# Router products from chunks of x2 inside the branch stage, with the root and the offset applied afterwards

## The reference, cut to what matters

```
x  = x + g1 * (merged @ w_out)                       # x2, 320 x 1024
h2 = rms_norm(x, norm2_w) * (1 + sc2) + sh2          # sc2, sh2 per sequence
logits = h2 @ w_router + b_router                    # 320 x 32
top_val, top_idx = top_k(logits, 4)
top_w = softmax(top_val)
y  = sum over the 4 experts of top_w * expert(h2)    # clamped SwiGLU, 32 experts
x  = x + g2 * y ; then a final RMSNorm
```

## Time and profile before

| | |
|---|---|
| median of 3 runs | 1829.15 us (1824.63 to 1832.14) |
| the profiled execution's own time | 1827.68 us |
| its span | 1825.7 us |
| PE busy | 1624.7 us (89%) |
| DVE busy | 766.2 us (42%) |
| ACT busy | 410.9 us (23%) |
| POOL busy | 126.7 us (7%) |

### The profile page before, as it was taken

One profiled execution on the slowest core, in us unless ns is written; L12 is line 12 of the kernel. 1 busy time (PEld: TensorE's weight loads), 2 busy tenths in 40 slices (PEclk: granted clock), 3 DMA queues, 4 the chain that ended last, 5 costly groups with the idle time before them and its releaser, 6 DMA issues. The chain is left out here.

```text
span 1825.7 us, 24039 instructions
## 1 busy us (share of the span) xinstructions
PE 1624.7 (89%) x8449; PEld 872.7 (48%) x8450; DVE 766.2 (42%) x1531; ACT 410.9 (23%) x792; POOL 126.7 (7%) x208
## 2 busy tenths in 40 slices
PE   6997898899978999878998988999989999899995
PEld 3775584686855676564333333333323333333332
DVE  2355332344152001284446265364462653644626
ACT  3234112111001200123223133132231331312313
POOL 0211120211210420010000000000000000000000
PEclk9899998999589999978999999999999999999997
DMA  9362208113018533305989999999999999999991
GB/s 314 143 221 74 74 1 314 55 47 104 0 46 243 193 131 146 138 1 238 424 356 425 426 416 425 412 425 425 415 425 417 414 424 393 425 426 409 426 401 43
DMA packets 115088, 494.61 MB, mean 271 GB/s; under 512 B 9947, under 2 KB 27548, under 8 KB 65831
## 3 DMA queue, kind: packets, MB, share of 16 engines
q1 hardware_dynamic: 113050, 491.21, 67.4%
q10 hardware_dynamic: 1984, 2.64, 0.5%
HBM read 487.39 MB, written 6.43 MB: 270 GB/s over the span
## 5 line engine op out<-in xcount | busy, mean ns | idle before, releaser
L761 PE MATMUL ps_mix<-hT,ring 128*128 128x320 f32 x896 | 263.7, 452 | 19.4 <-DVE ring L1234 9.7
L761 PEld LDWEIGHTS ps_mix<-hT,ring 128*128 128x128 f32 x896 | 175.7, 199 | 99.1 <-issue 16.4
L1905 PE MATMUL ps_moe<-ring,hT_moe 128*64 128x512 f32 x672 | 157.2, 627 | 2.6 <-ACT hT_moe L1848 2.6
L1905 PE MATMUL ps_moe<-ext,xg 128*64 128x512 f32 x672 | 147.0, 594 | 0.4 <-issue 0.2
L1905 PE MATMUL ps_moe<-ring,xg 128*64 128x512 f32 x672 | 147.1, 594 | 0.0
L2091 DVE TENSOR_SCALAR hid<-ps_moe 128x256 f32<-128x256 f32 (+1 forms) x96 | 48.8, 509 | 154.4 <-ACT hid L1840 111.5
L2077 DVE TENSOR_SCALAR gate<-ps_moe 128x1024 f32<-128x1024 f32 x32 | 39.2, 1225 | 148.5 <-ACT hid L1835 99.9
L1905 PEld LDWEIGHTS ps_moe<-ring,hT_moe 128*64 128x64 f32 x672 | 54.4, 145 | 98.3 <-issue 97.9
L2063 DVE TENSOR_TENSOR work<-work,ps_moe 128x640 f32<-128x640 f32 x128 | 99.4, 818 | 1.4 <-PE ps_moe L1921 0.3
L1905 PEld LDWEIGHTS ps_moe<-ext,xg 128*64 128x64 f32 x672 | 48.3, 137 | 94.2 <-issue 91.9
L1905 PEld LDWEIGHTS ps_moe<-ring,xg 128*64 128x64 f32 x672 | 47.1, 137 | 91.0 <-issue 91.0
(11 more groups left out here) (409 smaller groups left out, 2225.0 us busy)
## 6 DMA issues: line engine op xcount, KB each, us to landing
ext<-in_w_gate SPq DMA_DIRECT2D x128, 1024.0 KB, 15.6
ring<-in_w_up SPq DMA_DIRECT2D x128, 1024.0 KB, 15.9
ring<-in_w_down SPq DMA_DIRECT2D x128, 1024.0 KB, 12.2
ring<-in_w_in SPq DMA_DIRECT2D x18, 2048.0 KB, 8.3
ring<-in_w_ada SPq DMA_DIRECT2D x12, 2048.0 KB, 10.9
ext<-in_state_gdn_rec SPq DMA_DIRECT2D x8, 512.0 KB, 7.3
out_rec_sample<-ext SPq DMA_DIRECT2D x8, 512.0 KB, 6.1
ring<-in_w_branch_b SPq DMA_DIRECT2D x2, 2048.0 KB, 10.3
```

Of the source, the lines that this page charges most:

```text
L761: last = nc.tensor.matmul(out, ring[:, place(i), k, P * j:P * j + P], rhs[:, k, :], start=k == 0, stop=k == NC - 1)
L1905: ends = [nc.tensor.matmul(ps[MID * a:MID * a + MID, bank + blk, :], lhs(blk, c), w[:, k, HALF * a:HALF * a + HALF], start=c == 0 and not ...
```

## The change

PE no longer multiplies h2T with the router's matrix. In the branch stage DVE makes, for each chunk, x2 times its weights w (`hx`, kept in the place of `gb`), and PE multiplies these chunks with `wr` on the four strips: four products after unit 4 of `wo`, four after the last unit and ahead of the last square. After the reciprocal DVE multiplies the result by `rstd` into the first chunk of `yacc` (which is `lrow` now; the copy by ACT is gone). In the routing stage PE forms sh2 @ w_router for the nine sequences (`shw`), and adds it to the tokens with `seqT`, a 0/1 matrix of sequence by token that POOL makes first. The prompt's offset of h2 is added by ACT instead of DVE. POOL clears `yacc` in the routing stage, after the logits.

```diff
 # branches
+        def logits(c0):
+            pe.wait_ge(hx_s, c0 + NSTRIP + HX0)
+            for q in range(NSTRIP):
+                last = nc.tensor.matmul(ps[STRIP * q:STRIP * q + STRIP, 6, 0:T], wr[:, c0 + q, :], hx[:, c0 + q, :],
+                                        start=c0 == 0, stop=c0 > 0)
+            last.then_inc(lg_t, 1)
...
             if kind == "wo" and c >= 1:
                 add_square(c - 1)
+            if (kind, c) == ("wo", NSTRIP):
+                pe.wait_ge(ld, 32)
+                logits(0)
+        logits(NSTRIP)
         add_square(NC - 1)
...
+                if c == 0:
+                    link(nc.vector.tensor_scalar(gw2[:], SC2, 1.0, None, ALU.add))
+                    nc.vector.tensor_tensor(gw2[:], gw2[:], n2w.unsqueeze(2).to_broadcast([P, NC, NSEQ]), ALU.mult).then_inc(gw_s, 1)
...
+                dve.wait_ge(dve_s, taken(n)[1])
+                nc.vector.tensor_scalar(hx[:, c, 0:SEQ], x2T[:, c, 0:SEQ], gw2[:, c, 0:1], None, ALU.mult)
+                nc.vector.tensor_tensor(seq_view(hx[:, c, SEQ:T]), seq_view(x2T[:, c, SEQ:T]),
+                                        gw2[:, c, 1:NSEQ].unsqueeze(2).to_broadcast([P, NS, ST]), ALU.mult).then_inc(hx_s, 1)
...
         nc.vector.reciprocal(rstd[:], rstd[:]).then_inc(rs_s, 1)
+        dve.wait_ge(rs_s, 2)
+        dve.wait_ge(lg_t, 2)
+        nc.vector.tensor_tensor(yacc[:, 0, :], ps[:, 6, 0:T], rstd[:], ALU.mult)
 # experts, POOL
+                nc.gpsimd.memset(seqT, 1.0).then_inc(seq_s, 1)
...
+                nc.gpsimd.affine_select(out=seqT[:, 0:SEQ], in_=seqT[:, 0:SEQ], compare_op=ALU.is_equal, fill=0.0,
...
+                pool.wait_ge(lg_t, 3)
+                nc.gpsimd.memset(yacc[:], 0.0)
 # experts, ACT
-                nc.scalar.activation(lrow[:], ps[:, 6, 0:T], ACT.Copy).then_inc(lrow_s, 1)
+                for c in range(NC):
+                    act.wait_ge(hm_s, 9 * 16 + c + 1)
+                    nc.scalar.activation(h2T[:, c, 0:SEQ], h2T[:, c, 0:SEQ], ACT.Identity, bias=SH2[:, c, 0:1]).then_inc(h_s, 1)
 # experts, PE
+                for c in range(NC):
+                    last = nc.tensor.matmul(ps[0:NSEQ, 0, 0:E], SH2[:, c, :], wr[:, c, :], start=c == 0, stop=c == NC - 1)
+                last.then_inc(shw_t, 1)
...
+                    nc.tensor.matmul(o, lrow[:, t0:t0 + n], expert_row[:], start=True, stop=False)
+                    last = nc.tensor.matmul(o, seqT[:, t0:t0 + n], shw, start=False, stop=True)
...
+                        if tau == 0:
+                            pe.wait_ge(h_s, k + 1)
 # experts, DVE
+                dve.wait_ge(shw_t, 1 + SHW0)
+                nc.vector.tensor_copy(shw, ps[0:NSEQ, 0, 0:E]).then_inc(shw_s, 1)
...
-                        nc.vector.tensor_scalar(h2T[:, c - 1, 0:SEQ], h2T[:, c - 1, 0:SEQ], SH2[:, c - 1, 0:1], None,
-                                                ALU.add).then_inc(h_s, 1)
```

More of the change, by code:

```diff
@@ L1239, in branches @@
 def branches(nc, t, st, sb, sem, ring, ident, ones, gnw, short, adaT, hT, oT, zT, tails, x2T, xrow, order, norm, load_slot,
-             wait_slot, load_piece, yacc, brow, rstd, wr, br):
+             wait_slot, load_piece, yacc, brow, rstd, wr, br, n2w):
     ps = st.enter_context(nc.psum_tensor("ps_br", [P, 8, 512], F32))
@@ L1250, in branches @@
     sq = sb("sq_b", [P, 2, T], st)
-    ld, rows_d, bias_s = sem("rt_ld"), sem("rt_rows_d"), sem("rt_bias_s")
+    ld, rows_d, bias_s, lg_t = sem("rt_ld"), sem("rt_rows_d"), sem("rt_bias_s"), sem("rt_lg_t")
     sq_s, sum_t, mean_s, log_s, rs_s = norm
@@ L1257, in branches @@
     st_out = sem("st_out")
-    G1 = adaT[:, 16:24, :]
+    G1, SC2 = adaT[:, 16:24, :], adaT[:, 32:40, :]
+    gw2 = zT[:].rearrange("p h t -> p (h t)")[:, 0:NC * NSEQ].rearrange("p (c s) -> p c s", c=NC)
+    hx = gb
+    gw_s, hx_s = sem("c_sb"), sem("st_t")
+    GW0, HX0 = 1, 1
     def wait_taken(eng, n):
@@ L1310, in _ @@
             bias_step(nc.gpsimd.tensor_copy(brow[rows], whole[rows]))
-        nc.gpsimd.memset(yacc[:], 0.0)
     @block.scalar
@@ L1452, in experts @@
             h2T = room[:, 0:NC * T].rearrange("p (c t) -> p c t", c=NC)
-            lrow = room[:, 3200:3520]
+            lrow = yacc[:, 0, :]
             gw = room[:, 3520:3592].rearrange("p (c s) -> p c s", c=NC)
@@ L1485, in experts @@
             sq_s, sum_t, mean_s, log_s, rs_s = norm
+            seqT = room[0:NSEQ, 3600:3600 + T]
+            shw = room[0:NSEQ, 3920:3920 + E]
+            shw_t, shw_s, seq_s = sem("st_s"), sem("vec_s"), sem("silu_c")
+            SHW0, SEQ0 = 1, 1
             seat_s, SEAT0 = exp_s, 1
@@ L1490, in _ @@
             def _(pool):
+                nc.gpsimd.memset(seqT, 1.0).then_inc(seq_s, 1)
+                pool.wait_ge(seq_s, 1 + SEQ0)
+                nc.gpsimd.affine_select(out=seqT[:, 0:SEQ], in_=seqT[:, 0:SEQ], compare_op=ALU.is_equal, fill=0.0,
+                                        base=0, pattern=[[0, SEQ]], channel_multiplier=1).then_inc(seq_s, 1)
+                nc.gpsimd.affine_select(out=seqT[:, SEQ:T].rearrange("p (s t) -> p s t", s=NS),
+                                        in_=seqT[:, SEQ:T].rearrange("p (s t) -> p s t", s=NS), compare_op=ALU.is_equal, fill=0.0,
+                                        base=-1, pattern=[[-1, NS], [0, ST]], channel_multiplier=1).then_inc(seq_s, 1)
                 nc.gpsimd.iota(iota[:], pattern=[[1, SPAN]], base=0, channel_multiplier=0,
@@ L1536, in _ @@
             def _(pe):
-                pe.wait_ge(ld, 32)
-                pe.wait_ge(lrow_s, BIAS_STEPS + 1)
[L1539 to L1546, removed]
+                for c in range(NC):
+                    last = nc.tensor.matmul(ps[0:NSEQ, 0, 0:E], SH2[:, c, :], wr[:, c, :], start=c == 0, stop=c == NC - 1)
+                last.then_inc(shw_t, 1)
+                pe.wait_ge(row_s, P // E + 1)
+                pe.wait_ge(seq_s, 3 + SEQ0)
+                pe.wait_ge(lrow_s, BIAS_STEPS + 1)
+                pe.wait_ge(shw_s, 1 + SHW0)
                 for tau, (t0, n) in enumerate(TILE):
-                    last = nc.tensor.matmul(ps[0:n, 7, 256 + E * tau:256 + E * tau + E], lrow[:, t0:t0 + n], expert_row[:],
-                                            start=True, stop=True)
+                    o = ps[0:n, 7, 256 + E * tau:256 + E * tau + E]
+                    nc.tensor.matmul(o, lrow[:, t0:t0 + n], expert_row[:], start=True, stop=False)
+                    last = nc.tensor.matmul(o, seqT[:, t0:t0 + n], shw, start=False, stop=True)
                 last.then_inc(lg_t, 1)
@@ L1608, in _ @@
                 nc.vector.tensor_tensor(samples, samples, SH2[:, :, 1:NSEQ].unsqueeze(3).to_broadcast([P, NC, NS, ST]), ALU.add)
[L1609 to L1614, removed]
-                        nc.vector.tensor_scalar(h2T[:, c - 1, 0:SEQ], h2T[:, c - 1, 0:SEQ], SH2[:, c - 1, 0:1], None,
-                                                ALU.add).then_inc(h_s, 1)
-                dve.wait_ge(lg_t, 2)
+                for c in range(NC):
+                    nc.vector.scalar_tensor_tensor(out=h2T[:, c, 0:SEQ], in0=x2T[:, c, 0:SEQ], scalar=gw[:, c, 0:1],
+                                                   in1=rstd[:, 0:SEQ], op0=ALU.mult, op1=ALU.mult).then_inc(hm_s, 1)
+                dve.wait_ge(lg_t, 3)
                 dve.wait_ge(ld, 32)
```

6 lines of the change are left out of this document (3 added, 3 removed).

## The result

| | before | after |
|---|---|---|
| median of the runs | 1824.82 us (1823.03 to 1833.39, 7 runs) | 1840.02 us (1831.12 to 1842.27, 7 runs) |
| ratio | | 1.0058 [1.003, 1.0085] |
| profiled execution, its span | 1827.68, 1825.7 us | 1841.44, 1839.3 us |

The ratio is worked out from all runs and not from the two medians, whose quotient is 1.0083. The median of before is also the lowest of the four groups of runs of the kernel before in this document; the other three lie between 1828.51 and 1830.16 us.

What follows compares the result with a forecast made beforehand. Weights set the expert stage, so only the chain from the branch stage's last unit to the gather counts: +1.85 - 2.1 = -0.25 us, from 1827.68 to 1827.4 us profiled, median 1829; range 1824.5 to 1834.5 us.

Steps and rivals of the forecast that it cites:

- an expert stage of another length: Expert stage, behind the gather: a changed length was listed as a sign that the forecast is wrong; no size given.
- Steps 1 to 3: Branch stage: first four strips, last four strips and the product with rstd add +1.85 us (1.4 to 5.1).
- step 2: End of the branch stage: hx and the last four strips delay the last square by +0.7 us (0.4 to 2.3).
- rival D: Branch stage: the strips do not overlap, +3.2 us on the sum, 1832 us; chance 0.03.
- step 1: Branch stage: the first four strip products lengthen PE's unbroken run by 0.6 us (0.5 to 2.2).
- Step 4: Routing stage: DVE's copy of shw waits 2.6 us for small products; sample tokens start +1.9 us later (1.4 to 2.5).
- Step 5: Routing stage: DVE's sixteen chunk instructions become eight, 3.2 us instead of 5.35; DVE through at 8.65 instead of 8.91.
- Step 6: Routing stage: expert_row at 6.45, twelve PE records in 1.7 to 2.2 us, bias at 9.1, 2.2 us earlier (1.4 to 2.5).
- Step 7: Routing stage: ACT's offsets take 0.42 us each; h2l starts at 12.2 instead of 14.37, win 2.1 us (1.4 to 2.5).
- rival B: Routing stage: PE's logits, turns and counting run at 1.2 GHz throughout, +4.2 us on the sum, 1833 us; chance 0.12.
- Rival C: Gather: it runs at 1.2 GHz; all 240 further products at half clock make +28 us, 1857 us; chance 0.03.
- Rival A: Chain to the gather: gain arrives whole, step 4 under 2.1 us, tail under 0.4, counting earlier; -3 us, 1826; chance 0.08.

Runs made afterwards that it cites:

- the 45: The kernel before with 45 already satisfied waits behind the last square, as many instructions as the change adds to PE's program; median 1837.69 us, ratio 1.0052.
- the repeat: The changed kernel run once more, unaltered; median 1834.75 us, ratio 1.0028 against the kernel before.
- equal place: Address directive behind the last square puts both kernels' expert code at one place of a page; before 1828.37 us (offset 56), changed 1831.43 us (offset 44).
- the late strips: The changed kernel with the address directive at offset 44 and the last four strip products behind the last square; median 1828.78 us, ratio 0.9995.

## Why the prediction was wrong

**The step that failed** is the first paragraph's: "a microsecond won or lost on the chain from the last unit of the branch stage to the gather counts in full, and nothing else in this change can." The length of PE's program counted too. As mere instructions the 45 moved the block's start by 1.0 us at most; their price, 7 to 8 us in the profiles, fell due some 75 to 105 us later, in code that the diff doesn't touch. The prediction did list "an expert stage of another length" as a sign of error, and left 0.04 for a drift of that stage, without a mechanism. The row was there to be read: a wait of 1.51 us for `issue` in the first experts, under a DMA share of 1.01, of which the prediction asked nothing since the change left that code alone.

The first half of that sentence failed as well, at a smaller price: the chain did not count in full. The +0.5 at the gather was +0.1 at the gate of expert 0, in the first profile and in the repeat. With 45 waits +0.9 became 0.0, and with the late strips -1.2 became -3.0, each against the kernel before. PE's granted clock during the gather differed each time.

How far the time fell outside the range was partly chance: the first profile lost 3.8 us ahead of `wo`, and the repeat's median of 1834.75 us lies only 0.25 above the range's end. The cause of the experts' loss is not in doubt by that, since it came again in the repeat's profile and with 45 waits alone.

**The chain** was close: forecast -0.25 (-1.1 to +3.7), +0.5 in the first profile and in the repeat, +0.6 at equal place. (By its own rows it is 33 us long from the last unit at 764.74, not 45; nothing hangs on that.) By terms:

- Steps 1 to 3, the branch: +1.85 forecast, +2.1 measured. The last square stands 2.13 us behind the start of its chunk, before 1.43: the 0.7 of step 2; the product with `rstd` 0.49. The strips overlapped, as the earlier trace rows said, 0.74 us for eight records, so rival D falls. What is left for step 1 is 0.9 (forecast 0.6).
- Step 4 was oversized: the copy of `shw` came at t = 1.1, not 2.6. Sixteen small records took 1.01 us, 0.063 each; both rows that I scaled from were too dear. The 9 and 16 columns in the earlier trace rows are those that are moved; 128 columns of weights are loaded there each time, and here 9. The sample tokens started at 1.7, not 3.4.
- Step 5: 3.25 us for eight chunks against 3.2, but through at t = 7.0 for the reason just given.
- Step 6: `expert_row` at 5.5 (6.45 forecast), but its twelve records took 3.0 us at half clock, not 1.7 to 2.2. The two errors cancel: the bias at 8.6, forecast 9.1. POOL and PE were late, as said.
- Step 7: offsets 0.41 each, as forecast. h2l started 2.65 us earlier, but at half clock the turns spread it, and the win was 1.6 instead of 2.1. This is rival B, half of it: the turns ran at 1.2 GHz as it said, but the counting did not fall behind by 4.2.

Rival C did not come: over the gather's first 4 us the granted clock is 0.53 before and 0.59 after, and the gate of expert 0 moves by 0.1. Rival A asked for all of step 7 and didn't come either.

## What to carry to other kernels

An edit's price includes the instructions that it adds to an engine whose later code is entered for the first time while DMA is full: look for waits for nothing visible beside instruction fetches, in the stage behind the edit too. Before a difference under 1% is put down to an edit, compare both versions with the later code at the same place of a page, or try a few places; here the place alone was worth 11 us, and the edit at equal place 0.1 in the profile. And small products in front of a critical run are priced with the clock that they leave behind: strips 0.7 us later gave 3 us of profile back, which the runs bear out only weakly.

## What the runs showed of the hardware that was not expected

- A wait that is already satisfied is not free on PE: 211 of them, with two conditions each, filled 22.02 us, 0.104 each. From the last square to the next block's start there are 3.5 us before, and 4.6, 22.0 and 27.5 with 45, 211 and 256 waits. That 45 of them moved the block's start by only 1.0 fits, since they fill idle time first.
- A page of instructions that comes late stopped PE for 2.6 to 5.1 us at a time while weights kept the DMA engines at 1.01, and PE went on 1.4 to 1.6 us behind the end of the 16 KB packet. In the changed kernel none was fetched from 895 to 1790 us.
- Products that load nine columns of weights and move 32 took 0.063 us a record at a granted clock of 0.50, a third of the 0.183 of records that load 128 columns and move 16 at the same clock.
